# Routed experts' gate and up weights handled in two channel halves of each place of the ring

## The chip, the cores and the metric

The kernel runs on one core of a Trainium2 chip. The metric is the device time of one execution in microseconds (us); before the change it is the median of 3 runs. A profile of one execution gives the span from the first to the last instruction and the rows shown below.

## The reference

Two transformer blocks of width 1024 are applied to 256 tokens (batch 1). The first has two kinds of attention and then a mixture of 64 routed experts with 8 chosen for each token, beside one shared expert. The second has two gated feed-forward layers of width 2816 around another mixture of attentions. All is in float32. The change concerns the routed experts:

```python
def swiglu(x, w_gate, w_up, w_down):
    return (jax.nn.silu(x @ w_gate) * (x @ w_up)) @ w_down
...
    def body(acc, bidx):
        ...
        e = blk_expert[bidx]
        ye = swiglu(xt[rows], w_gate_e[e], w_up_e[e], w_down_e[e]) * wr[:, None]
        return acc.at[rows].add(ye.astype(acc.dtype)), None
```

Each expert has a gate and an up matrix of 1024x256 and a down matrix of 256x1024, 1 MiB each, so that 192 MiB of weights are read for this stage alone.

## The kernel before

The stage of the routed experts lies between about 285 and 767 us of the profiled execution. The rows (tokens) of an expert are gathered by a product with a 0/1 matrix; experts are put in order of size, and the work is cut into 28 turns, numbered 0 to 27. A turn fills the 128 rows of a PE pass: kinds P and B take one load, which is a pair of experts, kind Q takes two loads, which is four experts with 32 rows each. `KINDS = "PPQPPBPPQPPPBPPQPPBPPPPBPPPQ"`, so turns 2, 8, 15 and 27 take two loads and there are 32 loads of 6 MiB, numbered 0 to 31.

The weights go through `ring`, which has two places; load n goes to place n % 2. A place holds six units of 1 MiB (`UNIT` = 2048 floats on each of 128 partitions): gate of expert 0 and 1, up of expert 0 and 1, down of expert 0 and 1. In a gate or up unit each partition holds 8 channels of 256 numbers, 8 KB that lie together in memory, as well.

Everything waits by semaphores, and each engine runs its list in order. The sync engine (SP) issues all weight transfers on one queue, which serves them in that order. For a load it waits until PE has finished gate and up of the turn that used the place before (`used_gu`), and issues four transfers (L603); then for the down products of that turn (`y_ps`), and issues two (L612). Turn 2 takes load 2 with its down weights before load 3; later turns of two loads issue both loads' gate and up first, then both loads' down. Before a turn's transfers SP reads the experts' numbers from `order_i`, which is there at about 285 us; loads 0 and 1 go to fixed experts and are in flight before that.

PE in turn s (`body(s)`): `rows_gate_up(s)` (L2272: for each of the 8 channels, one product for each expert of the turn, into bank 4, 32 products for a pair), then gathering for a later turn (`fill`, L2247), adding the last turn's result to the tokens (`scatter`, L2309), `pick_t` (L2261), the transpose `rows_t` (L2282), and `rows_down(s)` (L2297). Turns 2 and 8 begin with the shared expert's products (L2210), turns 3 and 9 with its down part (L2222, L2230). ACT and DVE do the activation and the gating (L954, L1459), once all eight channels are summed. In the source:

```python
                if load >= 2:
                    sp.wait_ge(used_gu, 4 * (TURN_OF[load - 2] + 1))
...
                    for k in range(len(places) // 2):
                        pe.wait_ge(landed_gu[(load + k) % 2], 64 * ((load + k) // 2 + 1))
```

Of the kernel before, what the change touches and what calls it, by code (L numbers as in the profile page):

```python
# [127 lines left out]
def build(nc, a, out):  # L128
    ctx = ExitStack()
    with ctx:  # L130
# [190 lines left out]
        def bank(i):  # L321
            return ps[i // 2][:, i % 2, :]
# [15 lines left out]
        class Stream:  # L338
# [3 lines left out]
            def __init__(self, tag):  # L342
# [12 lines left out]
        in_ = {n: sem("in_" + n) for n in ("c", "x", "con", "ident", "bada", "relb", "bucket", "rpb",  # L355
                                           "tb", "nb", "mods", "g2r", "t1", "n1", "tw", "nw", "wrt", "rbias", "gains", "post",
# [3 lines left out]
        c_silu, c_wide = sem("c_silu"), sem("c_wide")  # L360
# [4 lines left out]
        tb_ps, tb_sb = sem("tb_ps"), sem("tb_sb")  # L365
# [10 lines left out]
        rt_tot, rt_flag, ordered = sem("rt_tot"), sem("rt_flag"), sem("ordered")  # L376
        w_back, w_there = sem("w_back"), sem("w_there")
        tok_hi = sem("tok_hi")
        landed_gu = [sem(f"landed_gu{i}") for i in range(2)]
# [89 lines left out]
        def if_over(eng, body):  # L469

            eng.wait_ge(rt_flag, 1)
# [16 lines left out]
        def _(sp):  # L488
# [63 lines left out]
            def spread_rows(r):  # L552

                sp.wait_ge(ada_rows, r + 1)
                sp.wait_ge(in_["n1"], 16)
                for j in range(4):
                    dst = mods[2 * r + j // 2][:, j % 2 * 512:j % 2 * 512 + 512]
                    for q in range(4):
                        sp.dma_start(dst[q:P:4, :], mod_rows[32 * j:32 * j + 32, :]).then_inc(in_["mods"], 16)

            for t in range(N_WIN):
                load_dense(G_WIN + t, w_in[:, :, t * 512:(t + 1) * 512])
                if t == 1 or t >= 3:
                    k = DC + 2 * max(t - 2, 0)
                    load_ada(k)
                    load_ada(k + 1)
                if t == 8:
                    spread_rows(1)
                if t == 5:

                    sp.wait_ge(in_["tw"], 16)
                    sp.dma_start(mb_bias, bass.AP(t_dram.tensor, 127, [[NH * BX - 1, P], [BX, NH], [1, T]]))\
                        .then_inc(in_["tb"], 16)
# [8 lines left out]
            sp.dma_start(w_rt, a["w_router"][0].rearrange("(p c) n -> p c n", c=DC)).then_inc(in_["wrt"], 16)  # L582
            sp.dma_start(rbias, a["router_bias"].to_broadcast([P, E])).then_inc(in_["rbias"], 16)
# [72 lines left out]
            sp.wait_ge(used_gu, 4 * N_TURN)  # L656
            sp.dma_start(pre1, a["ffn1_pre_g_2"].to_broadcast([P, D])).then_inc(in_["gains"], 16)
            def na_tables():

                sp.wait_ge(in_["nw"], 16)  # L660
# [48 lines left out]
        def _(pool):  # L709
# [42 lines left out]
            def double_roots():  # L752
# [15 lines left out]
            pool.wait_ge(tb_sb, 1)  # L768
            pool.dma_start(t_one, t_bias).then_inc(in_["t1"], 16)
            pool.wait_ge(in_["t1"], 16)  # L770
            pool.dma_start(t_dram, t_one.unsqueeze(0).to_broadcast([P, NH, BX])).then_inc(in_["tw"], 16)
# [3 lines left out]
                .then_inc(in_["rpb"], 16)  # L775
            pool.wait_ge(in_["rpb"], 16)
            pool.dma_start(n_one, rpb_pad).then_inc(in_["n1"], 16)
            pool.wait_ge(in_["n1"], 16)
            pool.dma_start(n_dram, n_one.unsqueeze(0).to_broadcast([64, NH, NR])).then_inc(in_["nw"], 16)
# [21 lines left out]
        def _(act):  # L801
# [128 lines left out]
            def sparse_phase():  # L930
# [78 lines left out]
            act.activation(c_sil, c_col, ACT.Silu).then_inc(c_silu, 1)  # L1009
# [10 lines left out]
            act.dma_start(relb_in[0:32, :], a["rel_bias_t"]).then_inc(in_["relb"], 16)  # L1020
            act.dma_start(bucket_in, a["buckets"]).then_inc(in_["bucket"], 16)
# [264 lines left out]
        def _(dve):  # L1286
# [116 lines left out]
            def sparse_phase():  # L1403
# [42 lines left out]
                def body(s):  # L1446
# [7 lines left out]
                    if s == 1:  # L1454
                        dve.wait_ge(rt_tot, 1)
                        dve.tensor_copy(over_i[0:1, 0:1], bank(7)[0:1, 0:1]).then_inc(rt_flag, 1)
# [50 lines left out]
            dve.wait_ge(c_silu, 1)  # L1507
            dve.tensor_copy(c_bc[:, :, :], c_sil.unsqueeze(2).to_broadcast([P, DC, 32])).then_inc(c_wide, 1)
# [60 lines left out]
            def sb_negabs(g):  # L1569
                z = of_group(z_sb, g)  # L1570
                dve.wait_ge(sb_zc, 2 * g + 2)
                if g == 0:
                    dve.wait_ge(in_["t1"], 16)
                dve.scalar_tensor_tensor(out=of_group(l_sb, g), in0=z, scalar=-1.0, in1=z, op0=ALU.mult, op1=ALU.min)\
                    .then_inc(sb_ab, 1)
# [56 lines left out]
            for j in range(N_WIN):  # L1632
                if j == 1:
                    dve.wait_ge(tb_ps, 1)
                    dve.tensor_copy(t_bias, bank(0)[0:NH, 0:BX]).then_inc(tb_sb, 1)
# [79 lines left out]
            dve.wait_ge(in_["rbias"], 16)  # L1715
# [82 lines left out]
            def over():  # L1798
# [6 lines left out]
                dve.wait_ge(w_back, 1)  # L1805
                dve.tensor_copy(w_over, bank(4)[:, 0:P].rearrange("p (b e) -> p b e", b=TB)).then_inc(w_there, 1)
                dve.wait_ge(w_there, 1)
# [193 lines left out]
        def _(pe):  # L2001
# [231 lines left out]
            def sparse_phase():  # L2233
# [31 lines left out]
                def rows_gate_up(s):  # L2265

                    _, places, load, groups, _ = TURNS[s]
                    for k in range(len(places) // 2):
                        pe.wait_ge(landed_gu[(load + k) % 2], 64 * ((load + k) // 2 + 1))
                    for c in range(DC):  # L2270
                        for i, (r, pair, j, at_) in enumerate(groups):
# [3 lines left out]
                            if c == DC - 1:  # L2275
                                last.then_inc(used_gu, 4 // len(groups))
# [39 lines left out]
                def body(s):  # L2316
# [23 lines left out]
                    if s == 1:  # L2340
# [3 lines left out]
                            .then_inc(rt_tot, 1)  # L2344
                        pe.wait_ge(rt_flag, 1)
# [158 lines left out]
            pe.wait_ge(c_wide, 1)  # L2504
# [106 lines left out]
            for j in range(N_WIN):  # L2611
# [12 lines left out]
                if j == 1:  # L2624
                    pe.wait_ge(in_["relb"], 16)
                    pe.wait_ge(in_["bucket"], 16)
                    pe.matmul(bank(0)[0:NH, 0:BX], relb_in, bucket_in, start=True, stop=True).then_inc(tb_ps, 1)
                if j >= 2:
                    pe.wait_ge(ev_v, EV_V[G_WIN + j - 2])
                if j == FIRST:  # L2630
                    pe.wait_ge(in_["con"], 16)
                    pe.wait_ge(tb_sb, 1)
# [32 lines left out]
            pe.wait_ge(in_["wrt"], 16)  # L2665
# [36 lines left out]
            def over():  # L2702
# [3 lines left out]
                pe.transpose(bank(4)[:, 0:P], w_past, ident).then_inc(w_back, 1)  # L2706
                pe.wait_ge(w_there, 1)
# [122 lines left out]
```

## Time and profile before

| | us |
|---|---|
| median of 3 runs | 1321.71 |
| lowest and highest run | 1319.38, 1323.28 |
| span of the profiled execution | 1317.2 |
| busy in it: PE, DVE, ACT | 1224.0, 541.9, 445.1 |

The page gives the profiled execution by its span only; the 4.5 us between span and median lie before the first and behind the last instruction, or between executions. Matmuls are pipelined and overlap in the rows, so a sum of busy times is no path. A chain of waits is followed back from the last instruction; a piece of it that reads "DMA" runs from the issue of the transfer to its landing.

### The profile page before, as it was taken

The page shows a single profiled execution, that of the slowest core. Times are in us where ns is not written, and L with a number is a line of the kernel's source. Part 1 is how long each engine was busy: PE and PEld are TensorE (multiplying, and loading weights), DVE is VectorE, ACT ScalarE, POOL GpSimd, SP SyncE. Part 2 cuts the span into 40 slices and gives each one's busy share as a digit, 9 for nine tenths or more (in the row PEclk, how much of TensorE's full clock was granted, in tenths as well). Part 3 has the DMA queues.
Part 4 walks back from the last instruction along what each step waited for, and adds up shares of the span by engine and source line. Part 5 has one row for each costly group of instructions (what it writes and reads, how often), then busy time and mean ns, then how long its engine had stood idle before and what let it go on. Part 6 is the DMA issues. An engine that isn't in the chain of part 4 may idle for free.

```text
span 1317.2 us, 16742 instructions
## 1 busy us (share of the span) xinstructions
PE 1224.0 (93%) x6726; PEld 855.7 (65%) x6726; DVE 541.9 (41%) x812; ACT 445.1 (34%) x657; POOL 44.5 (3%) x66
## 2 busy tenths in 40 slices
PE   4999999989999999789999779999999988999998
PEld 2877777754445444344455257888889867788886
DVE  1555546651111122111122165554566545544454
ACT  1345445321211122111122044444345545444332
POOL 0000000000000000000000020300010001000000
PEclk9899999989999999889999889999999979999999
DMA  9996655768999999999999998465615106455540
GB/s 372 363 363 230 223 200 184 286 250 351 372 421 421 412 421 421 405 398 421 421 420 421 407 270 259 158 212 185 228 46 192 64 1 224 156 196 187 186 137 32
DMA packets 115315, 359.54 MB, mean 273 GB/s; under 512 B 15092, under 2 KB 62629, under 8 KB 84334
## 3 DMA queue, kind: packets, MB, share of 16 engines
q1 hardware_dynamic: 113520, 352.71, 70.9%
q0 software_dynamic: 320, 3.46, 0.7%
q10 hardware_dynamic: 1406, 2.42, 0.6%
q8 instruction: 48, 0.79, 0.2%
q14 instruction: 21, 0.17, 0.0%
HBM read 355.37 MB, written 4.50 MB: 273 GB/s over the span
## 4 chain that ended last, share of the span: by engine, by line
PE 79%; DMA 10%; DVE 5%; ACT 2%; SPq 1%; issue 1%; POOL 0%; DVEq 0%; POOLq 0%; ACTq 0%
PE bank L2029 29%; PE bank L2272 14%; PE bank L2169 9%; DMA ring<-in_w_up_e 8%; PE bank L2297 6%; PE bank L2116 4%; PE bank L2247 4%; PE bank L2309 3%; DMA att<-in_w_ada 2%; PE bank L2380 1%; PE bank L2402 1%; PE bank L2085 1%; PE bank L2045 1%; PE bank L2158 1%; DMA raw_g<-in_ffn_w_gu 1%
## 5 line engine op out<-in xcount | busy, mean ns | idle before, releaser
L1301 DVE TENSOR_TENSOR g_lo<-raw_g,g_hi 128x2048 fp32r<-128x2048 f32 (+2 forms) x84 | 192.7, 2295 | 112.7 <-ACT g_hi L824 56.9
L2029 PE MATMUL bank<-g_hi,xt_hi 128*128 128x512 f32 (+1 forms) x576 | 231.2, 401 | 7.1 <-DVE xt_lo L1307 2.6
L2272 PE MATMUL bank<-ring,xg 128*64 128x512 f32 (+1 forms) x1152 | 205.1, 616 | 27.1 <-DMA ring<-in_w_up_e 27.1
L2029 PE MATMUL bank<-g_hi,xt_lo 128*128 128x512 f32 (+1 forms) x576 | 225.1, 391 | 0.0
L2029 PE MATMUL bank<-g_lo,xt_hi 128*128 128x512 f32 (+1 forms) x576 | 224.1, 389 | 0.0
L2272 PEld LDWEIGHTS bank<-ring,xg 128*64 128x64 f32 (+1 forms) x1152 | 64.7, 129 | 163.1 <-issue 159.4
L2029 PEld LDWEIGHTS bank<-g_hi,xt_hi 128*128 128x128 f32 x576 | 108.6, 189 | 35.5 <-issue 12.3
L2029 PEld LDWEIGHTS bank<-g_hi,xt_lo 128*128 128x128 f32 x576 | 108.4, 188 | 23.0
L2029 PEld LDWEIGHTS bank<-g_lo,xt_hi 128*128 128x128 f32 x576 | 108.6, 189 | 20.5
L824 ACT ACTIVATE g_hi<-raw_g 128x2048 fp32r<-128x2048 f32 (+3 forms) x42 | 78.2, 1865 | 77.5 <-PE bank L2029 39.4
L2297 PE MATMUL bank<-ring,a_t 128*64 128x512 f32 (+1 forms) x576 | 102.6, 598 | 1.4 <-DVE pickT L1412 0.9
L1459 DVE SCALAR_TENSOR_TENSOR arena<-arena,w_row_of,bank 128x256 f32<-128x256 f32 x28 | 13.4, 480 | 203.6 <-ACT arena L954 203.6
L822 ACT ACTIVATE g_hi<-raw_g 128x2048 fp32r<-128x2048 f32 x44 | 84.1, 1913 | 20.3 <-DMA raw_g<-in_ffn_w_gu 11.8
L954 ACT ACTIVATE arena<-bank 128x256 f32<-128x256 f32 x28 | 10.8, 385 | 222.4 <-PE bank L2272 222.4
L1444 DVE TENSOR_TENSOR y_lo<-bank,y_hi 128x512 fp32r<-128x512 f32 x56 | 38.7, 692 | 104.3 <-ACT y_hi L940 104.3
L1321 DVE TENSOR_TENSOR d_lo<-raw_d,d_hi 128x2048 fp32r<-128x2048 f32 x20 | 48.5, 2423 | 45.7 <-ACT d_hi L868 45.7
L2297 PEld LDWEIGHTS bank<-ring,a_t 128*64 128x64 f32 (+1 forms) x576 | 30.4, 125 | 53.0 <-issue 48.8
L2169 PE MATMUL bank<-d_hi,at_hi 128*128 128x512 f32 x160 | 62.5, 390 | 0.0
L2169 PE MATMUL bank<-d_hi,at_lo 128*128 128x512 f32 x160 | 62.3, 389 | 0.0
L2169 PE MATMUL bank<-d_lo,at_hi 128*128 128x512 f32 x160 | 62.2, 389 | 0.0
L940 ACT ACTIVATE y_hi<-bank 128x512 fp32r<-128x512 f32 x56 | 33.4, 597 | 70.4 <-PE bank L2297 70.4
L868 ACT ACTIVATE d_hi<-raw_d 128x2048 fp32r<-128x2048 f32 x20 | 38.3, 1917 | 52.5 <-PE bank L2169 52.5
(370 smaller groups left out, 1665.6 us busy)
## 6 DMA issues: line engine op xcount, KB each, us to landing
ring<-in_w_gate_e SPq DMA_DIRECT2D x64, 1024.0 KB, 12.8
ring<-in_w_up_e SPq DMA_DIRECT2D x64, 1024.0 KB, 16.8
ring<-in_w_down_e SPq DMA_DIRECT2D x64, 1024.0 KB, 16.2
raw_g<-in_ffn_w_gu SPq DMA_DIRECT2D x44, 1024.0 KB, 9.4
raw_g<-in_w_in SPq DMA_DIRECT2D x26, 1024.0 KB, 7.7
raw_d<-in_ffn_w_down SPq DMA_DIRECT2D x22, 1024.0 KB, 5.0
ada_d<-in_w_ada SPq DMA_DIRECT2D x16, 1024.0 KB, 7.0
raw_g<-in_w_out SPq DMA_DIRECT2D x8, 1024.0 KB, 5.3
```

What stands on the lines that cost most here:

```text
L822: act.activation(dst, raw_gated(g, u), ACT.Copy).then_inc(S.hi_g, 1)
L824: act.activation(g_hi[:, u, 0:cols], raw_dense(g, u)[:, 0:cols], ACT.Copy).then_inc(S.hi_g, 1)
L1301: dve.tensor_tensor(lo, raw, hi.bitcast(F32), ALU.subtract).then_inc(S.lo_g, 1)
L1321: dve.tensor_tensor(d_lo[:, :], raw_d[:, d % 2, :], d_hi[:, :].bitcast(F32), ALU.subtract)\
L1444: dve.tensor_tensor(lo, bank(5 + m), hi.bitcast(F32), ALU.subtract).then_inc(y_v, 1)
L2029: last = pe.matmul(out_, src[s][:, c, b * P:(b + 1) * P], w((g_hi, g_lo)[m], i), start=start and i == 0 and k == 0, stop=stop and i == len ...
L2116: last = pe.matmul(bank(banks[m // 2])[:, (m % 2) * T:(m % 2 + 1) * T], (g_hi, g_lo)[w][:, u, c * 512 + m * P:c * 512 + (m + 1) * P], (xt_ ...
L2169: last = pe.matmul(bank(2 * b + m), a_hl[i][:, c, b * P:(b + 1) * P], d_hl[w][:, c * D + m * 512:c * D + (m + 1) * 512], start=False, stop ...
L2247: last = pe.matmul(fill_bank(n)[:, i * 4 * ROWS:(i + 1) * 4 * ROWS], tok[k][:, b, c, :], pick[:, q % 2, b, :], start=k == 0 and b == 0 and ...
L2272: last = pe.matmul(bank(4)[r, :].rearrange("p (g n) -> p g n", g=2), xg[:, s // 2 % 2, c, at_:at_ + r.stop - r.start], gate_up_raw(pair, j ...
L2297: last = pe.matmul(bank(5 + m)[r, :], a_t[:, c, r], down_raw(pair, j, c, m), start=c == 0, stop=c == 1, skip_group_check=True)
L2309: last = pe.matmul(bank(2 * b + m), pickT[:, s % 2, b * P:(b + 1) * P], t[:, m * 512:(m + 1) * 512], start=False, stop=s == N_TURN - 1 and ...
```

## The change

The gate and up part of a load is issued as eight transfers of half a unit: first channels 0 to 3 of gate and up of both experts, then channels 4 to 7. Each half has its own wait of SP for the place (the half turn before that frees it), its own semaphore for the landing, and its own wait of PE, ahead of channel 0 and ahead of channel 4. PE reports the place's halves used after channel 3 and after channel 7, so that `used_gu` counts 8 a turn, and those that wait for a turn's end wait for 8 s + 8. A partition's piece in one transfer is 4 KB where it was 8 KB. The down weights are loaded as before. In the same diff several semaphores elsewhere are merged (for example `c_silu` and `c_wide` into `c_ready`, and those of the router's weights and bias into `router`), with the counts waited for raised accordingly.

```diff
-        landed_gu = [sem(f"landed_gu{i}") for i in range(2)]
+        landed_gu = [[sem(f"landed_gu{i}{j}") for j in range(2)] for i in range(2)]
...
             def load_gate_up(load, pair):
 
-                if load >= 2:
-                    sp.wait_ge(used_gu, 4 * (TURN_OF[load - 2] + 1))
-                for g, n in enumerate(("w_gate_e", "w_up_e")):
-                    for j in range(2):
-                        at_ = (2 * g + j) * UNIT
-                        sp.dma_start(ring[:, load % 2, at_:at_ + UNIT], one_row(n, pair[j], DC))\
-                            .then_inc(landed_gu[load % 2], 16)
+                for half in range(2):
+                    if load >= 2:
+                        sp.wait_ge(used_gu, 8 * TURN_OF[load - 2] + 4 * half + 4)
+                    for g, n in enumerate(("w_gate_e", "w_up_e")):
+                        for j in range(2):
+                            at_ = (2 * g + j) * UNIT + half * (UNIT // 2)
+                            sp.dma_start(ring[:, load % 2, at_:at_ + UNIT // 2],
+                                         one_row(n, pair[j], DC)[:, half * (UNIT // 2):(half + 1) * (UNIT // 2)])\
+                                .then_inc(landed_gu[load % 2][half], 16)
...
-            sp.wait_ge(used_gu, 4 * N_TURN)
+            sp.wait_ge(used_gu, 8 * N_TURN)
...
-                    act.wait_ge(used_gu, 4 * s + 4)
+                    act.wait_ge(used_gu, 8 * s + 8)
...
-            pe.wait_ge(in_["wrt"], 16)
+            pe.wait_ge(in_["router"], 32)
...
-                    for k in range(len(places) // 2):
-                        pe.wait_ge(landed_gu[(load + k) % 2], 64 * ((load + k) // 2 + 1))
                     for c in range(DC):
+                        for k in range(len(places) // 2 if c % (DC // 2) == 0 else 0):
+                            pe.wait_ge(landed_gu[(load + k) % 2][c // (DC // 2)], 64 * ((load + k) // 2 + 1))
                         for i, (r, pair, j, at_) in enumerate(groups):
                             last = pe.matmul(bank(4)[r, :].rearrange("p (g n) -> p g n", g=2),
                                              xg[:, s // 2 % 2, c, at_:at_ + r.stop - r.start], gate_up_raw(pair, j, c),
                                              start=c == 0, stop=c == DC - 1, skip_group_check=True)
-                            if c == DC - 1:
+                            if c % (DC // 2) == DC // 2 - 1:
                                 last.then_inc(used_gu, 4 // len(groups))
```

## Rows read from the trace of the kernel before

**Rows 1.** The page's head, and GB/s moved in 40 slices of the span.

```profile
span 1317.2 us, 16742 instructions
...
GB/s 372 363 363 230 223 200 184 286 250 351 372 421 421 412 421 421 405 398 421 421 420 421 407 270 259 158 212 185 228 46 192 64 1 224 156 196 187 186 137 32
```

**Rows 2.** The chain that ended last, whole span, shares by engine.

```profile
PE 79%; DMA 10%; DVE 5%; ACT 2%; SPq 1%; issue 1%; POOL 0%; DVEq 0%; POOLq 0%; ACTq 0%
```

**Rows 3.** PE's waits from 285 to 770 us: total, times, longest.

```profile
PE bank L2272 <- DMA ring<-in_w_up_e: 27.1, 7, 8.8
```

**Rows 4.** Windows: length, busy of PE, PEld, DVE, ACT, POOL, PEclk, DMA share, GB/s.

```profile
325.00:333.00 8.00, 8.00 (x74) 3.57 (x64) 0.48 (x1) 0.73 (x2) 0.00 (x0) 1.00 0.25 74
350.00:436.00 86.00, 83.63 (x506) 43.94 (x506) 16.50 (x48) 16.24 (x32) 0.00 (x0) 1.00 1.01 421
557.00:563.00 6.00, 6.00 (x48) 3.58 (x41) 0.48 (x1) 0.98 (x2) 0.00 (x0) 1.00 0.59 197
563.00:757.00 194.00, 181.03 (x1042) 85.67 (x1045) 35.62 (x97) 35.73 (x68) 0.00 (x0) 0.96 1.01 420
...
749.00:751.00 2.00, 2.00 (x13) 0.45 (x9) 0.00 (x0) 0.00 (x0) 0.00 (x0) 0.50 1.04 434
```

**Rows 5.** The chain in order of time, routed stage: start us, us, what.

```profile
310.73 13.52 DMA ring<-in_w_up_e
324.39 7.07 PE bank L2272 x64
...
606.34 7.00 PE bank L2272 x64
...
621.51 7.02 PE bank L2272 x32
...
735.83 12.50 DMA ring<-in_w_up_e
748.46 9.29 PE bank L2272 x64
```

**Rows 6.** The timeline at the stage's start and end: start us, us, instructions.

```profile
284.95 7.09 PE L2272 MATMUL bank<-ring,xg 128*64 128x512 f32 x32
...
292.27 0.89 SPq L603 DMA_DIRECT2D ring<-in_w_gate_e  x2
...
309.31 0.85 SPq L603 DMA_DIRECT2D ring<-in_w_gate_e  x2
...
321.78 0.29 DVE L1401 TENSOR_TENSOR arena<-arena,bank 128x128 f32<-128x128 f32 x1 [2.63 <-ACT arena L923]
...
335.99 3.64 PE L2297 MATMUL bank<-ring,a_t 128*32 128x512 f32 x32
...
760.53 3.64 PE L2297 MATMUL bank<-ring,a_t 128*32 128x512 f32 x32 [0.47 <-ACT a_t L958]
```

**Rows 7.** Issue to landing of L612's two transfers from 339.72, then from 741.56 us.

```profile
DMA to landing us min/median/max: 8.0/9.0/10.0
...
DMA to landing us min/median/max: 14.2/15.3/16.3
```

**Rows 8.** A window (columns of rows 4) in which `w_out_2` alone lands, in 4 KB pieces.

```profile
1010.00:1011.50 1.50, 1.50 (x16) 1.50 (x15) 1.14 (x1) 0.85 (x2) 0.00 (x0) 1.00 1.00 412
```

**Rows 9.** Transfers: count, KB each, median us to landing; 8 KB pieces first, then 4 KB.

```profile
raw_d<-in_ffn_w_down SPq DMA_DIRECT2D x22, 1024.0 KB, 5.0
...
raw_g<-in_w_out SPq DMA_DIRECT2D x4, 1024.0 KB, 4.9
...
arena<-in_w_down_sh SPq DMA_DIRECT2D x1, 512.0 KB, 9.8
d_sh<-in_w_down_sh SPq DMA_DIRECT2D x1, 512.0 KB, 10.9
```

**Rows 10.** SP's timeline where those two of 512 KB are issued.

```profile
233.08 0.43 SPq L632 DMA_DIRECT2D arena<-in_w_down_sh  x1
233.55 0.76 SPq L632 DMA_DIRECT2D d_sh<-in_w_down_sh  x1
```

More of the change, by code:

```diff
@@ L354, in build @@
         h_ready, x_ready = sem("h_ready"), sem("x_ready")
-        in_ = {n: sem("in_" + n) for n in ("c", "x", "con", "ident", "bada", "relb", "bucket", "rpb",
-                                           "tb", "nb", "mods", "g2r", "t1", "n1", "tw", "nw", "wrt", "rbias", "gains", "post",
+        in_ = {n: sem("in_" + n) for n in ("c", "x", "con", "ident", "bada", "buckets", "n_table",
+                                           "t_table", "tb", "nb", "mods", "g2r", "router", "gains", "post",
                                            "outg", "ff2g")}
@@ L359, in build @@
         set_up = sem("set_up")
-        c_silu, c_wide = sem("c_silu"), sem("c_wide")
+        c_ready = sem("c_ready")
         landed_ada = [sem(f"landed_ada{i}") for i in range(4)]
@@ L364, in build @@
         mod_col, w0_half = sem("mod_col"), sem("w0_half")
-        tb_ps, tb_sb = sem("tb_ps"), sem("tb_sb")
+        tb_made = sem("tb_made")
         ev_a, ev_v = sem("ev_a"), sem("ev_v")
@@ L469, in if_over @@
         def if_over(eng, body):
-            eng.wait_ge(rt_flag, 1)
+            eng.wait_ge(rt_beyond, 2)
             beyond = eng.value_load(over_i[0:1, 0:1], min_val=0, max_val=T * E)
@@ L554, in spread_rows @@
                 sp.wait_ge(ada_rows, r + 1)
-                sp.wait_ge(in_["n1"], 16)
+                sp.wait_ge(in_["n_table"], 32)
                 for j in range(4):
@@ L581, in _ @@
             sp.wait_ge(h_ready, 4)
-            sp.dma_start(w_rt, a["w_router"][0].rearrange("(p c) n -> p c n", c=DC)).then_inc(in_["wrt"], 16)
-            sp.dma_start(rbias, a["router_bias"].to_broadcast([P, E])).then_inc(in_["rbias"], 16)
+            sp.dma_start(w_rt, a["w_router"][0].rearrange("(p c) n -> p c n", c=DC)).then_inc(in_["router"], 16)
+            sp.dma_start(rbias, a["router_bias"].to_broadcast([P, E])).then_inc(in_["router"], 16)
             def moe_gate_up(s, it):
@@ L766, in _ @@
             roots(0, 2)
[L768 to L771, printed above, removed]
+            pool.wait_ge(tb_made, 2)
+            pool.dma_start(t_one, t_bias).then_inc(in_["t_table"], 16)
+            pool.wait_ge(in_["t_table"], 16)
+            pool.dma_start(t_dram, t_one.unsqueeze(0).to_broadcast([P, NH, BX])).then_inc(in_["t_table"], 16)
             link(pool.memset(rpb_pad, 0.0))
             pool.dma_start(rpb_pad.rearrange("h (r c) -> h r c", r=7)[:, :, 48:79], a["na_rpb_2"][0][:, 4:11, :])\
[L775 to L779, printed above, removed]
+                .then_inc(in_["n_table"], 16)
+            pool.wait_ge(in_["n_table"], 16)
+            pool.dma_start(n_one, rpb_pad).then_inc(in_["n_table"], 16)
+            pool.wait_ge(in_["n_table"], 32)
+            pool.dma_start(n_dram, n_one.unsqueeze(0).to_broadcast([64, NH, NR])).then_inc(in_["n_table"], 16)
             block_roots(1)
@@ L1008, in _ @@
             act.wait_ge(in_["c"], 16)
-            act.activation(c_sil, c_col, ACT.Silu).then_inc(c_silu, 1)
+            act.activation(c_sil, c_col, ACT.Silu).then_inc(c_ready, 1)
             squares(0, [x[:, b, :] for b in range(TB)], in_["x"], 16, lambda i: h[:, i, :])
@@ L1019, in _ @@
             act.dma_start(con[:, P:C_END], a["con"][:, P:C_END]).then_inc(in_["con"], 16)
-            act.dma_start(relb_in[0:32, :], a["rel_bias_t"]).then_inc(in_["relb"], 16)
-            act.dma_start(bucket_in, a["buckets"]).then_inc(in_["bucket"], 16)
+            act.dma_start(relb_in[0:32, :], a["rel_bias_t"]).then_inc(in_["buckets"], 16)
+            act.dma_start(bucket_in, a["buckets"]).then_inc(in_["buckets"], 16)
             bias_rows(1, ADA_ROUNDS)
@@ L1454, in body @@
                     if s == 1:
-                        dve.wait_ge(rt_tot, 1)
-                        dve.tensor_copy(over_i[0:1, 0:1], bank(7)[0:1, 0:1]).then_inc(rt_flag, 1)
+                        dve.wait_ge(rt_beyond, 1)
+                        dve.tensor_copy(over_i[0:1, 0:1], bank(7)[0:1, 0:1]).then_inc(rt_beyond, 1)
                     dve.wait_ge(sp_silu, s + 1)
@@ L1504, in attend2 @@
                     sm_finish(8 + s - 3)
-            dve.wait_ge(c_silu, 1)
-            dve.tensor_copy(c_bc[:, :, :], c_sil.unsqueeze(2).to_broadcast([P, DC, 32])).then_inc(c_wide, 1)
+            dve.wait_ge(c_ready, 1)
+            dve.tensor_copy(c_bc[:, :, :], c_sil.unsqueeze(2).to_broadcast([P, DC, 32])).then_inc(c_ready, 1)
             def ada_sum(r):
@@ L1633, in _ @@
                 if j == 1:
-                    dve.wait_ge(tb_ps, 1)
-                    dve.tensor_copy(t_bias, bank(0)[0:NH, 0:BX]).then_inc(tb_sb, 1)
+                    dve.wait_ge(tb_made, 1)
+                    dve.tensor_copy(t_bias, bank(0)[0:NH, 0:BX]).then_inc(tb_made, 1)
                 if j:
@@ L1714, in _ @@
                                          op0=ALU.mult, op1=ALU.add).then_inc(h_ready, 1)
-            dve.wait_ge(in_["rbias"], 16)
+            dve.wait_ge(in_["router"], 32)
             def sel01(b):
@@ L1804, in over @@
                 transposed(0, OV, 4)
-                dve.wait_ge(w_back, 1)
-                dve.tensor_copy(w_over, bank(4)[:, 0:P].rearrange("p (b e) -> p b e", b=TB)).then_inc(w_there, 1)
-                dve.wait_ge(w_there, 1)
+                dve.wait_ge(w_moved, 1)
+                dve.tensor_copy(w_over, bank(4)[:, 0:P].rearrange("p (b e) -> p b e", b=TB)).then_inc(w_moved, 1)
+                dve.wait_ge(w_moved, 2)
                 gated_phase("over", weight=w_over)
@@ L2343, in body @@
                         pe.matmul(bank(7)[0:1, 0:1], st[:, 52:53], ones[:, 0:1], start=True, stop=True)\
-                            .then_inc(rt_tot, 1)
-                        pe.wait_ge(rt_flag, 1)
+                            .then_inc(rt_beyond, 1)
+                        pe.wait_ge(rt_beyond, 2)
                     if more:
@@ L2503, in _ @@
             pe.wait_ge(set_up, 3)
-            pe.wait_ge(c_wide, 1)
+            pe.wait_ge(c_ready, 2)
             ada_chunks(0, 4)
@@ L2624, in _ @@
                 if j == 1:
-                    pe.wait_ge(in_["relb"], 16)
-                    pe.wait_ge(in_["bucket"], 16)
-                    pe.matmul(bank(0)[0:NH, 0:BX], relb_in, bucket_in, start=True, stop=True).then_inc(tb_ps, 1)
+                    pe.wait_ge(in_["buckets"], 32)
+                    pe.matmul(bank(0)[0:NH, 0:BX], relb_in, bucket_in, start=True, stop=True).then_inc(tb_made, 1)
                 if j >= 2:
@@ L2705, in over @@
                 pe.wait_ge(OV.xt_lo, 4)
-                pe.transpose(bank(4)[:, 0:P], w_past, ident).then_inc(w_back, 1)
-                pe.wait_ge(w_there, 1)
+                pe.transpose(bank(4)[:, 0:P], w_past, ident).then_inc(w_moved, 1)
+                pe.wait_ge(w_moved, 2)
                 pe.sem_inc(OV.used_d, 1)
```

12 lines of the change are left out of this document (6 added, 6 removed).

## Prediction

> **What bounds the kernel now.** I read the page's head first: the GB/s in slices of 33 us. From the 12th to the 22nd slice, the stage of the routed experts, the transfers run at 398 to 421 GB/s and nowhere else do they stay there [rows 1]. Then the chain's shares: PE 79%, DMA 10% [rows 2]; and PE's waits inside the stage: 27.1 us in 7 waits, all on `ring`, the longest 8.8 [rows 3]. So the chain runs mostly over PE, and still the gain to be had is not on PE. The windows show why: from 350 to 436 and from 563 to 757 us the DMA share is 1.01 at 420 to 421 GB/s [rows 4]. A load of 6 MiB (6.29 MB) takes 6.29 / 421 = 14.94 us; a turn of one load takes 621.51 - 606.34 = 15.17 us [rows 5]. The two are within 2% of each other. The four turns with two loads need 29.9 us of transfers and give PE about as much to do as the others, and there PE waits. Over 30 loads (2 to 31) the transfers need 30 x 14.94 = 448 us, of the 466 from their first issue at 292.27 to the last landing [rows 6, 7]: the stream of transfers is the bound, and what counts is when it starts, where it stops, and how fast a MiB goes.
>
> Where it stops in the profile: before 292.27 (SP waits for the end of turn 0's gate and up, 284.95 + 7.09 [rows 6]); 325 to 333 us at a share of 0.25; 557 to 563 us at 0.59, that is 2.5 us idle [rows 4]. The last landing is 741.99 + 16.3 = 758.3 [rows 7] (the second of the two is issued 0.4 us behind the first). PE's last down products start at 760.53, and what ended their wait was ACT's `a_t`, not the landing [rows 6].
>
> **The change, part by part.**
>
> *Earlier release.* The half of a plain turn's gate and up is 7.07 / 2 = 3.5 us. SP may issue channels 0 to 3 that much earlier. For load 2: 284.95 + 3.5 + 0.2 = 288.7 in place of 292.27. Load 3 likewise, 3.5 us ahead of its 309.31 [rows 6].
>
> *Turn 2.* It begins at 324.39, when load 3's last gate and up transfer lands (310.73 + 13.52) [rows 5]. PE itself is ready after the shared expert's gating, 321.78 + 0.29, say 322.2 [rows 6]. Half 0 of load 3 is issued at 305.8; behind the down weights of load 2, which are still issued when turn 0's down products end, near 302, and land near 310, its 2 MiB land near 316 and half 1 near 321, before PE needs it at 325.7. So turn 2 starts at 322.2: 2.2 us earlier. What is late next is load 4: its half 0 is issued at turn 2's middle, 325.9, in place of 331.7, and lies in the hole of 325 to 333; its down weights wait for turn 2's down products and (the end of 335.99 + 3.64 [rows 6]) and go out at 339.72 - 2.2 = 337.5, landing at 337.5 + 2.5 + 5.0 = 345.0. (2.5 us from issue to first data: a lone MiB lands after 5.0 us [rows 9], 2.5 of it data.) In the profile they landed at 340.15 + 10.0 = 350.2 [rows 7]. Of the 5.2 us gained, 2.2 is turn 2's start and 3.0 is that gate and up of load 4 no longer stand in the queue ahead of them.
>
> *From there the stream does not stop.* After 345.0 each half is freed well before its place in the queue comes up. The tightest is load 19, freed by turn 15 (loads 17 and 18): the stream would reach it at 345.0 + 14 x 15.16 = 557.2, and half of turn 15 is over near 547. Before, it was issued after the whole of turn 15, hence the 2.5 us idle at 557 to 563; these go.
>
> *The price: pieces of 4 KB.* A window in which only 4 KB pieces move shows 412 GB/s at a full share [rows 8], against 421 for 8 KB [rows 4]. Gate and up of a load: 4.194 MB / 412 = 10.18 us in place of 9.96; a load 15.16 in place of 14.94. Over the 27 loads from 5 to 31 that is +5.9 us. Bounds: from below, lone transfers of 1 MiB take 5.0 us in 8 KB pieces and 4.9 in 4 KB pieces [rows 9], so the price may be nothing; from above, the two transfers of 512 KB land at 233.08 + 9.8 = 242.9 and 233.55 + 10.9 = 244.5 [rows 9, 10], 1.6 us apart where 412 GB/s gives 1.27. That would be 216 halves x 0.33 = +71 us, but other traffic may lie in the one interval. I take the window, since it is a full queue as here.
>
> *The sum.* Before, from 350.2 to 758.3 are 408.1 us for 27 loads: 27 x 14.94 = 403.4, 2.5 idle, and 2.2 in late single landings. After: 345.0 + 27 x 15.16 (409.3) + 1.6 (of the 2.2, between none and all) = 755.9. Now the landing of the last down weights is what PE's last down products wait for: gate and up of load 31 land 10 us earlier, and with half 0 done by then turn 27's gate and up end near 750, `a_t` near 753. They start at 756.0, not at 760.53: **-4.5 us**. All that follows (the sums to the tokens, the norm, the feed-forward layer) hangs on them and moves along; its weights are issued after turn 27's gate and up and land earlier too. Span 1317.2 - 4.5 = 1312.7. The runs' median is 4.5 above the span, so 1321.7 - 4.5 = **1317.2**.
>
> *Costed at nothing.* Four more issues a load on SP: two take about 0.9 us, so ten take 4.7 of the 15.17 us of a turn; SP has nothing else to do, and no transfer is delayed while the stream is backed up. If it were starved, up to 1.9 us a load would show. PE's extra wait ahead of channel 4: behind it stand gathering, scatter, the transpose, and ACT and DVE after them; between the turns of two loads PE runs some us behind the landings, so it is met already; at turns 15, 16 and 27 it does stop PE, but there PE waits for the stream anyhow and now does half a turn's products meanwhile. The merged semaphores ask for the same events; where PE now waits for the router's bias too, that is issued right behind the weights, long before PE's output projection is done.
>
> *A rule of the skill against it.* The transfers of 1 MiB in the queue run at 421 GB/s [rows 4], and one alone takes 5.0 us for 2.5 us of data [rows 9]: in the queue the other 2.5 is hidden. The Trainium skill, DMA: Bandwidth & Descriptors, Bandwidth, advises batching to 1 MiB or more because each transfer has a fixed cost; by its figures (2.0 us plus bytes at 436 GB/s) splitting adds 8.0 us a load, an estimate of +216 us if nothing hid it. By the rows above nearly all of it is hidden.
>
> **The rivals.**
>
> *A. Halved transfers cost more than the window says (slower).* The place is each of the 216 half transfers from load 5 on; the price 216 x what each takes over 1.27 us. From 1.29 the gain is gone, from 1.31 the kernel is 0.3% slower; at 1.35 it would be 216 x 0.08 = +17 over my sum, 1334. For it speak the 1.6 us above; against it 412 GB/s in a full window and 4.9 beside 5.0 us. Chance 0.20.
>
> *B. 4 KB pieces cost nothing (more gain).* Then 27 x 0.22 = 5.9 more: 1311.3. For it: 4.9 beside 5.0; against: the window. The skill's same page (Specifications) has pieces from 512 B at line rate. By that rule it comes out so, 1311.3. Chance 0.12.
>
> *C. The clock takes the gain (no change).* After PE's 6.9 us of waiting ahead of turn 27 its granted clock is 0.50 in the window from 749 to 751 [rows 4], the lower of its two levels, 1.2 GHz, and gate and up take 9.29 us in place of 7.07 [rows 5]. After the change PE waits ahead of turn 27, again ahead of channel 4, and some 3 us for the last down weights. If the clock is low then, the last 3.64 us of products [rows 6] take up to twice that: -4.5 + 3.6 = -0.9, 1320.8. Against it: after the 2.3 us of waiting at turn 2 the products ran at 7.07 [rows 5]. Chance 0.13.
>
> *D. The start gains nothing.* If load 2's and 3's halves queue so that turn 2 starts as before, load 4's down weights land 3.0 earlier, not 5.2: 1319.4. Chance 0.10.
>
> My forecast keeps 0.45. **The numbers.** 0.3% is 4 us, about what a measurement can tell from none. The forecast's own spread, from lateness 0 to 2.2 and the window's 412 read as 410 to 415, is 1314 to 1320: six parts in ten of it beyond 4 us. Faster 0.45 x 0.6 + 0.12 + a little of C and D = 0.43; slower 0.20; the same 0.37. The range reaches from B, 1310, to A at 1.32 us a half, 1328.
>
> **What would show it.** In the profile after: L603's first issue near 288.7; turn 2's L2272 from 322.2; no window under a share of 1.00 from 345 to 755; 8 of L603 to a load, landing 1.27 us apart, 412 to 421 GB/s there; a last landing near 756 with L2297 waiting for `ring` from down weights, not for ACT. A mean of 1.31 us apart, or a stream that stops after 345, would make the prediction wrong.

## The result and the profile after

| | before | after |
|---|---|---|
| median of the runs compared, us | 1320.4 (19 runs) | 1324.1 (19 runs) |
| lowest and highest run, us | 1318.74, 1325.35 | 1322.32, 1326.04 |
| span of the profiled execution, us | 1317.2 | 1323.3 |
| own time of the profiled execution, us | not given | 1325.18 |

The ratio is 1.0021 with a 95% interval of 1.0012 to 1.003, so the changed kernel is slower by 0.21%, 1.6 to 4.0 us. (The two medians differ by 3.7 us; what follows goes by the ratio, 2.8 us.) That is within the 0.3% that the prediction counted as the same, but on the other side of no change from the 1317.2 us that it forecast. In the runs from here on, the profiled execution's own time is 1.8 to 1.9 us above its span. If that held before the change too, the execution profiled there took some 1319.1 us, an estimate, and of the 4.5 us between its span and the median 2.6 are only that it was a quick one.

The page's head and its GB/s by slices, which answer to [rows 1]:

```profile
span 1323.3 us, 17050 instructions
...
GB/s 371 341 368 242 209 206 189 253 309 338 385 413 412 413 414 412 413 412 412 413 414 412 406 268 238 155 217 182 230 51 191 64 1 222 151 197 183 186 141 32
```

From the 12th to the 22nd slice no slice falls below 412, where before two fell to 398 and 405; but none reaches 421 either. The stream no longer stops, and it runs slower throughout. The chain's shares by engine, against [rows 2]:

```profile
PE 70%; SPq 13%; DMA 7%; DVE 5%; ACT 2%; issue 2%; POOL 0%; DVEq 0%; POOLq 0%; ACTq 0%
```

SP's queue (SPq) has 13% of the chain where it had 1%. That isn't time in which SP waits for PE; the waits of SP and of PE inside the stage (total, times, longest) say so. SP before:

```profile
SPq L603 <- PE bank L2272: 187.9, 27, 16.2
SPq L612 <- PE bank L2297: 143.1, 24, 7.8
```

SP and PE after, L604 and L614 being the issues that were L603 and L612, L2274 and L2299 the products that were L2272 and L2297:

```profile
SPq L614 <- PE bank L2299: 36.5, 7, 8.3
SPq L604 <- PE bank L2274: 36.3, 12, 9.6
...
PE bank L2274 <- DMA ring<-in_w_up_e: 21.0, 7, 9.3
PE bank L2299 <- DMA ring<-in_w_down_e: 6.6, 3, 3.8
```

SP waited 331 us for PE and now waits 73. It may now issue well ahead, and the issues themselves stretch: two take 0.88 us together at 290.52, when the queue is empty, and one alone takes 1.03 us in the chain's rows below. That it is the full queue which holds them back is argued from that, not shown. PE's waits came to 27.1 us [rows 3] and are 27.6 now: some for gate and up went, 6.6 for down weights came. The windows that answer to [rows 4] (the same columns):

```profile
350.00:436.00 86.00, 84.53 (x511) 43.67 (x508) 16.52 (x48) 16.63 (x33) 0.00 (x0) 1.00 1.02 413
439.00:547.00 108.00, 99.63 (x568) 48.36 (x566) 20.59 (x56) 21.41 (x41) 0.00 (x0) 0.98 1.02 412
563.00:745.00 182.00, 169.56 (x970) 80.47 (x970) 34.12 (x90) 34.89 (x67) 0.00 (x0) 0.99 1.02 413
...
762.50:765.00 2.50, 2.42 (x12) 0.68 (x16) 0.00 (x0) 0.00 (x0) 0.00 (x0) 0.50 1.07 355
765.00:767.00 2.00, 2.00 (x16) 0.63 (x12) 0.07 (x1) 0.60 (x1) 0.00 (x0) 0.50 1.10 349
```

The DMA share is 1.02, a full stream, and moves 412 to 413 GB/s where it moved 420 to 421. The last two rows belong to the end of the stage, when transfers for the next layer are under way already; they are shown for the granted clock. The chain there, in order of time:

```profile
739.48 1.03 SPq L614
740.60 1.04 SPq L614
741.73 20.71 DMA ring<-in_w_down_e
762.44 0.14 issue
762.58 6.63 PE bank L2299 x32
```

The last down weights land at 741.73 + 20.71 = 762.44 us, PE stands idle for them, and its last down products take 6.6 us, where they took 3.64 [rows 6]: their granted clock is 0.50, the lower level of 1.2 GHz. (They are 16 products in 32 rows: the trace keeps two rows for one product in float32. Likewise gate and up of a pair are 16 products in 32 rows, not 32 products.)

**Where the stage starts.** Its first product is at 286.63 us, 1.7 later than the 284.95 of before [rows 6]. In the other profiles of this study it lies between 284.8 and 287.8, and four kernels that have the merged semaphores too start within 0.3 us of the kernel before. So I take it for scatter of single profiles and subtract it ("less 1.7") when the two are compared:

| us | predicted | profile after, less 1.7 |
|---|---|---|
| first L604 issue | 288.7 | 290.52 - 1.7 = 288.8 |
| turn 2 starts | 322.2 | 323.89 - 1.7 = 322.2 |
| down weights of load 4 landed | 345.0 | 349.3 - 1.7 = 347.6 |
| last down weights landed | 755.9 | 762.44 - 1.7 = 760.7 |
| last down products take | 3.64 | 6.56 |
| they end | 759.6 | 769.14 - 1.7 = 767.4 |

A single profile doesn't bear the last digit of this. The kernels with four loads halved (below) are alike up to the last turn; in their two profiles the stage starts at 285.18 and at 286.65 us, and turn 2 at 323.83 and 323.93. Differences of this table that are below some 1.5 us show little.

The spans of the two profiles differ by 6.1 us: 1.7 ahead of the stage's first product, 3.3 from there to the end of the last down products, and 1.1 behind them. This account explains the 3.3. The stretch behind is 553.0 us long before the change and 553.9 to 557.2 in the ten experiments' profiles. Whether the one profile of before is a quick one there, or something that all the changed kernels share costs time, was not settled.

In between PE ran ahead as meant. Turn 16 starts each half when that half has landed (the first two rows), at 568.71 where the whole began at 573.11, and turn 17 starts at 585.38 where it started at 591.06 (all times here as read, without the 1.7):

```profile
568.71 3.65 PE L2274 MATMUL bank<-ring,xg 128*64 128x512 f32 x16 [1.48 <-DMA ring<-in_w_up_e]
573.72 3.65 PE L2274 MATMUL bank<-ring,xg 128*64 128x512 f32 x16 [1.36 <-DMA ring<-in_w_up_e]
585.38 5.21 PE L2274 MATMUL bank<-ring,xg 128*64 128x512 f32 x21
```

But most of the lead of 5.7 us is given back: turn 27 starts at 747.54 instead of 748.46 [rows 5], after PE has waited 9.3 us for the stream. A lead of PE was worth nothing here, where the stream sets the end.

### The profile page after: what moved, and what is told of

It reads as the page before. It is cut to its first block, busy times and chain, and to the rows that moved or that the text cites. A ratio compares the mean times of both kernels' runs of the same rounds, so it can differ in the third digit from the quotient of the medians.

```text
span 1323.3 us, 17050 instructions
## 1 busy us (share of the span) xinstructions
PE 1231.3 (93%) x6723; PEld 858.7 (65%) x6726; DVE 542.2 (41%) x812; ACT 445.6 (34%) x657; POOL 45.4 (3%) x66
## 4 chain that ended last, share of the span: by engine, by line
PE 70%; SPq 13%; DMA 7%; DVE 5%; ACT 2%; issue 2%; POOL 0%; DVEq 0%; POOLq 0%; ACTq 0%
PE bank L2031 29%; SPq L604 9%; PE bank L2171 9%; PE bank L2274 7%; DMA ring<-in_w_down_e 5%; PE bank L2299 5%; PE bank L2118 4%; SPq L614 3%; PE bank L2249 2%; PE bank L2311 2%; PE bank L2047 1%; PE bank L2382 1%; PE bank L2404 1%; DMA arena<-in_w_ada 1%; PE bank L2087 1%
## 5 line engine op out<-in xcount | busy, mean ns | idle before, releaser
L2274 PE MATMUL bank<-ring,xg 128*64 128x512 f32 (+1 forms) x1152 | 203.7, 611 | 22.9 <-DMA ring<-in_w_up_e 21.0
L2274 PEld LDWEIGHTS bank<-ring,xg 128*64 128x64 f32 (+1 forms) x1152 | 61.8, 127 | 160.2 <-issue 146.5
L2299 PE MATMUL bank<-ring,a_t 128*64 128x512 f32 (+1 forms) x576 | 105.6, 620 | 7.5 <-DMA ring<-in_w_down_e 6.6
L826 ACT ACTIVATE g_hi<-raw_g 128x2048 fp32r<-128x2048 f32 (+3 forms) x42 | 78.2, 1865 | 77.7 <-PE bank L2031 39.4
L2299 PEld LDWEIGHTS bank<-ring,a_t 128*64 128x64 f32 (+1 forms) x576 | 31.5, 128 | 60.8 <-issue 57.6
```

What stands on the lines that cost most here:

```text
L826: act.activation(g_hi[:, u, 0:cols], raw_dense(g, u)[:, 0:cols], ACT.Copy).then_inc(S.hi_g, 1)
L2274: last = pe.matmul(bank(4)[r, :].rearrange("p (g n) -> p g n", g=2), xg[:, s // 2 % 2, c, at_:at_ + r.stop - r.start], gate_up_raw(pair, j ...
L2299: last = pe.matmul(bank(5 + m)[r, :], a_t[:, c, r], down_raw(pair, j, c, m), start=c == 0, stop=c == 1, skip_group_check=True)
```

## The experiments

Ten kernels were run, each compared with the kernel before on the same chip. Ratios and gains in us are to it, with the 95% interval behind the ratio.

**The semaphores and counts alone.** The changed kernel's merged semaphores and `used_gu` counting 8 a turn, with no load halved (`HALVED_LOADS = ()`, in the form shown under "four loads halved" below).

> The changed kernel with its merged semaphores and its count of 8 a turn, but each gate and up transfer whole (1 MiB, 8 KB pieces), waited for and given back whole. Theory 1 (all of the loss lies in the routed stage) expects the time of the kernel before, within 0.1%. The rival (the stage begins 1.7 us later in the changed kernel's profile because merged semaphores make something wait) expects 1.7 us or 0.13% more than before.

Measured 1321.39 us, 1.0007 (0.999 to 1.0023); windows 421, 419 and 421 GB/s. So these parts of the diff cost 0.9 us, from -1.3 to +3.0: nothing that can be told, as priced, though the rival's 1.7 us isn't excluded either.

**Half transfers with whole waits.** Nothing of the half turns' gain is left, only the price of the eight transfers:

```diff
-                        sp.wait_ge(used_gu, 8 * TURN_OF[load - 2] + 4 * half + 4)
+                        sp.wait_ge(used_gu, 8 * TURN_OF[load - 2] + 8)
...
-                        for k in range(len(places) // 2 if c % (DC // 2) == 0 else 0):
-                            pe.wait_ge(landed_gu[(load + k) % 2][c // (DC // 2)], 64 * ((load + k) // 2 + 1))
+                        for k in range(len(places) // 2 if c == 0 else 0):
+                            for half in range(2):
+                                pe.wait_ge(landed_gu[(load + k) % 2][half], 64 * ((load + k) // 2 + 1))
```

> The changed kernel with transfers in two channel halves of 4 KB pieces, but both halves' place waited for at the turn's end and both landings waited for ahead of channel 0: the price without the gain. At 413 GB/s, as in the changed kernel's profile, against 421, a load of 6.29 MB takes 0.3 us more, 27 loads 8.2 us; the last down landing had 2.2 us in hand before, and PE's last down products at the low clock would cost 2.9: 8.2 - 2.2 + 2.9 = +9 us over before. If the prediction's own price holds (0.22 us a load) +6.6.

Measured 1337.14 us, 1.0118 (1.0093 to 1.0144): **+15.6 us**, far more than the 5.9 of the prediction's sum. Its windows (columns as above):

```profile
350.00:436.00 86.00, 84.63 (x470) 44.73 (x470) 16.50 (x48) 16.25 (x32) 0.00 (x0) 0.98 1.02 413
439.00:547.00 108.00, 104.80 (x611) 51.67 (x604) 18.79 (x51) 20.22 (x39) 0.00 (x0) 0.99 0.99 395
563.00:745.00 182.00, 175.30 (x1022) 84.26 (x1024) 33.21 (x90) 34.75 (x66) 0.00 (x0) 0.97 1.00 403
563.00:573.00 10.00, 9.72 (x66) 2.90 (x67) 0.00 (x0) 0.11 (x1) 0.00 (x0) 0.74 0.81 337
```

Where nothing stops the stream it runs at the 413 GB/s of the changed kernel; around the turns of two loads it also stops, since those turns' places come free late. It stops for longer than in the kernel before, behind turn 8 and behind turn 15:

```profile
443.00:448.00 5.00, 5.00 (x43) 2.53 (x36) 0.48 (x1) 0.80 (x2) 0.00 (x0) 1.00 0.38 120
570.00:575.00 5.00, 5.00 (x42) 2.77 (x35) 0.48 (x1) 0.98 (x2) 0.00 (x0) 1.00 0.38 137
```

These are some 6 us without transfers, where the kernel before lost 2.5 behind turn 15 [rows 4] and about 0.4 behind turn 8 (a share of 0.89 from 436 to 439 us). Load 4's down weights also land 4.6 us later, at 354.76. So the price has several parts: the rate, longer stops and a later start.

**Count or size.** Two kernels, both with whole waits, take the two properties of a half transfer apart. The first keeps eight transfers a load and pieces of 8 KB, by giving each transfer every second partition; the second keeps four transfers of 1 MiB, each written as two pieces of 4 KB a partition, into the two halves of a place laid out half by half:

```diff
+                    part = slice(half, P, 2)
...
+                            sp.dma_start(ring[part, load % 2, at_:at_ + UNIT], one_row(n, pair[j], DC)[part, :])\
```

> Eight transfers of 512 KB a load in whole 8 KB pieces, waits whole as in e2_pieces, but each transfer takes every second partition, so that all 128 partitions are spread over as before (e3_rows, with 64 neighbouring partitions a transfer, moved at 221 to 243 GB/s and so told nothing of the number of transfers). Theory 1 (the size of the pieces costs) expects the kernel before, +0 to +1 us. Theory 2 (the number of transfers costs) expects +16 us, the time of e2_pieces.

```diff
+                        dst = ring[:, load % 2, 0:4 * UNIT].rearrange("p (h i n) -> p h i n", h=2, i=4)[:, :, 2 * g + j, :]
+                        sp.dma_start(dst, one_row(n, pair[j], DC).rearrange("p (h n) -> p h n", h=2))\
```

> The opposite: four transfers of 1 MiB a load as before, waits whole, but each partition's 8 KB go to two places of 4 KB (the ring's gate and up part is laid out half by half). Theory 1 expects e2_pieces, +16 us or, for the 4 KB packets alone (163 ns for 4 KB against 314 for 8 KB, 0.3 us a load), +8 to +12. Theory 2 expects the kernel before.

The count alone: 1324.27 us, 1.0022 (1.0006 to 1.0038), +2.9 us, above the 0 to 1 that was expected. The size alone: 1331.07 us, 1.0079 (1.006 to 1.0097), +10.4 us, as expected. The window from 350 to 436 us of the one and then of the other:

```profile
350.00:436.00 86.00, 83.99 (x501) 44.14 (x500) 16.50 (x48) 16.25 (x32) 0.00 (x0) 1.00 1.01 421
```

```profile
350.00:436.00 86.00, 81.88 (x494) 43.73 (x494) 16.50 (x48) 16.25 (x32) 0.00 (x0) 1.00 1.02 413
```

In this window twice as many transfers run at the rate of before; pieces half as long do not, in transfers of whatever number. So the rate is a matter of the piece's length, and with it two thirds of the price: 10.4 of the 15.6 us, and the count's 2.9 make 13.3. Neither figure is rate alone: from 563 to 573 us both kernels stop (shares of 0.95 and 0.81). At 413 against 421 GB/s, 27 loads take 7.8 us more, an estimate; the rest of the 10.4 is not taken apart.

**Eight transfers of 64 neighbouring partitions.** My first attempt at "count alone", with `part = slice(half * (P // 2), (half + 1) * (P // 2))`.

> As e2_pieces, eight transfers of 512 KB a load, but each is 64 partitions of whole 8 KB pieces. Theory 1 (the size of the pieces costs) expects the time of the kernel before, +0 to +1 us. Theory 2 (the number of transfers costs: SP's queue was full at 11 to 13 outstanding, and one DMA engine some us behind the others) expects the time of e2_pieces, +9 us.

Measured 1692.78 us, 1.2827 (1.2773 to 1.2881). Nothing like it was expected, and it says nothing about the count, since the rate broke down altogether:

```profile
350.00:436.00 86.00, 54.94 (x292) 25.47 (x292) 8.90 (x24) 9.75 (x19) 0.00 (x0) 0.82 0.91 221
```

**What wins the 13 us back.** Between half transfers with whole waits (+15.6) and the changed kernel (+2.8) lie SP's wait by halves and PE's wait by halves. One kernel keeps the first alone, with PE's whole wait as in the diff above; the other keeps PE's alone, with SP's whole wait.

> SP waits by halves as in the changed kernel, PE waits for both halves ahead of channel 0. If the early issue of transfers is what wins back the 13 us between all halves with whole waits (1337.1) and the changed kernel (1324.1): within 2 us of 1324. If PE's wait by halves wins them: near 1337. Mine: early issue wins most, since with it the queue holds work at every turn's end: 1325 to 1328, PE's wait by halves being worth at most the landing of four transfers (some 7 us) once, at the last turn.

> SP waits for the whole turn's end before all eight transfers of a load, PE waits by halves. If the early issue wins the 13 us: near 1337. If PE's wait by halves does: near 1324. Mine: 1331 to 1335; the stream still stops at the start of the stage and where a turn takes two loads, since nothing is issued before a turn's end.

SP's alone: 1326.69, 1.0041 (1.0025 to 1.0057). PE's alone: 1327.08, 1.0044 (1.0032 to 1.0056). Each wins back about 10 of the 13 us, SP's as expected; PE's I had expected to win 2 to 6. The window from 563 to 573 us shows it, SP's alone first, then PE's alone:

```profile
563.00:573.00 10.00, 8.02 (x62) 4.85 (x61) 3.40 (x10) 3.15 (x6) 0.00 (x0) 1.00 1.02 377
```

```profile
563.00:573.00 10.00, 7.29 (x48) 2.39 (x48) 1.38 (x2) 1.20 (x2) 0.00 (x0) 1.00 1.03 407
```

Either keeps the stream from stopping (share 1.02 and 1.03, against 0.81). PE's wait by halves must do it another way, as I read the program: the turn begins earlier, so it ends and frees the whole place earlier. The two gains are for the most part one gain, the stop, and can't be added.

**The clock at the end.** The changed kernel with 26 products of constants put ahead of the last down products (`warm(26, 7)` in turn 27), which keep PE at work while it would wait. They are added work, and show as 52 rows.

> The changed kernel with 26 products of 128x128 into the unused bank 7 ahead of the last turn's wait for its down weights, whose result nobody reads. If the lower clock of the last 32 down products (6.56 us where they took 3.64) is part of the loss, 2 to 3 us less than the changed kernel; if not, the same as the changed kernel or up to 1 us more.

Measured 1325.14 us, 1.0035 (1.002 to 1.005), where 2 to 3 us less than the changed kernel were expected if the clock was part of the loss. The timeline:

```profile
759.03 5.97 PE L2019 MATMUL bank<-con 128*128 128x128 f32 x52
764.93 3.64 PE L2299 MATMUL bank<-ring,a_t 128*32 128x512 f32 x32
```

With no idle time ahead of them the last down products take 3.64 us again, at a granted clock of 1.00. The cause of the 6.6 is thus shown; the gain isn't, because in this profile the weights landed at 763.85, 1.4 us later than in the other, and the added products ran 1.1 us beyond that.

**Four loads halved.** If the price is paid by each load and the gain made at few places, then only loads 2, 3 and 4 (the start) and 19 (behind turn 15) should be halved:

```diff
+HALVED_LOADS = (2, 3, 4, 19)
...
-                for half in range(2):
+                halves = 2 if load in HALVED_LOADS else 1
+                n_ = UNIT // halves
+                for half in range(halves):
```

> The changed kernel, but only loads 2, 3, 4 and 19 are halved (those ahead of which the stream stopped in the kernel before); the other 28 are whole. If the early release gains 5 us by load 4 and 2.5 at load 19, and the price lies in the pieces of the steady stretch, the last landing comes 7 us earlier at 421 GB/s: 6 to 8 us less than before (PE's last gate and up, still at the low clock, ends with its own 12 us behind the landing). If the gain was not there, the time of the kernel before.

Measured 1320.28 us, 1.0007 (0.999 to 1.0025): the price is gone, and of the 6 to 8 us expected no gain is left in the time. The windows of this kernel:

```profile
340.00:350.00 10.00, 9.90 (x38) 3.63 (x40) 0.49 (x1) 0.04 (x1) 0.00 (x0) 1.00 0.97 370
...
435.00:438.00 3.00, 3.00 (x27) 1.80 (x20) 0.48 (x1) 0.71 (x2) 0.00 (x0) 1.00 0.50 194
...
563.00:573.00 10.00, 10.00 (x67) 3.65 (x67) 2.70 (x8) 2.18 (x4) 0.00 (x0) 1.00 1.01 368
```

The down weights of load 4 landed at 349.4 us (350.2 before), although they were issued at 339.2, as the prediction has it: the 10 us in which they land move 370 GB/s, in the changed kernel 363, before 424. The stop behind turn 15 is gone, but behind turn 8, whose place load 11 takes, the stream now stops for 1.5 us (the second row; a share of 0.91 before, 1.01 in the changed kernel): the choice of loads missed it.

Part of the gain is there in the profile all the same. The last down weights land at 756.33 us where they landed at 758.28, and PE's last down products start at 757.76 where they started at 760.53, held up by ACT's `a_t`. What undoes it is the stretch behind the stage, 556.3 us against 553.0, of which the section on the result speaks.

**The same with the clock held.** The last kernel with 20 such added products ahead of turn 27's gate and up.

> e6_some with 20 products into the unused bank 7 ahead of the last turn's wait for its gate and up weights, so that PE does not idle there. If the clock's fall costs 2.2 us in the last turn's gate and up (9.29 us where 7.07), another 2 us less than e6_some; if it is hidden or falls anyway, the same.

Measured 1318.51 us, 0.999 (0.9978 to 1.0002), with an interval that still holds no change. Turn 27's gate and up took 9.6 us all the same. It is the lowest median of the study, and shown to be faster neither than the kernel before nor than the last one.

## Why the prediction was wrong

**Right.** The stream of transfers bounds the kernel; the first issue follows the stage's first product after 3.9 us (7.3 before), where 3.75 was forecast; turn 2 waits for the shared expert's gating and no longer for load 3; the stop behind turn 15 is gone (from 557 to 563 us the share is 1.01 where it was 0.59 [rows 4]); PE's last wait is for down weights; the merged semaphores cost nothing that shows; the stream stays full with eight issues a load, so SP is no limit; and twice the count keeps the rate of 421 GB/s in the window shown. The 2.2 us gained at turn 2 may be owed to the halves only in small part: with all loads whole it starts 37.5 us behind the stage's first product, where it is 37.3 with the halves and 39.4 in the profile of before.

**Wrong in three terms of the sum**, which together turn -4.5 into +3.3 us in the stage. The measured difference of the whole is 2.8, between 1.6 and 4.0.

1. *Landing of load 4's down weights, "337.5 + 2.5 + 5.0 = 345.0".* They were issued when predicted, 337.5 (339.21 less 1.7), and landed at 347.6: **2.6 us** lost. Load 4's own half transfers are all landed at 341.72, 2.5 us after the issue; the delay lies behind that. In the window from 340 to 350 us, at a share of 0.99, 363 GB/s move where 424 did, that is 0.61 MB or 1.4 us less. With load 5 whole, in the kernel with four loads halved, it is the same (370), so the length of what follows isn't the cause. Why transfers that meet an almost empty queue go at this rate is open; the term took two rows of lone transfers [rows 9] for a case that they don't cover. Rival D's 3.0 us earlier instead of 5.2 came nearest to the 2.6 that it is, but by another way: D had turn 2 start no earlier.

2. *"The price: pieces of 4 KB ... a load 15.16".* The prediction took 412 GB/s for the 4 KB pieces [rows 8] and 421 for the down weights, a mean of 415. The whole mix runs at 413, which leaves 409 for the 4 KB pieces, an estimate with 421 for the rest: 6.29 / 413 = 15.23 us a load, and from 349.3 to 762.44 us there are 413.1 us for 27 loads, 15.30 each. The terms were 409.3 + 1.6; measured are 411.2 at the windows' rate and 1.9 of lateness: **2.2 us** more. Over the half transfers this makes (15.30 - 4.98) / 8 = 1.29 us each, just where rival A put the point at which the gain is gone.

   What the lateness in both terms is made of can be seen closer. A transfer raises its semaphore in 16 steps as its parts land, and the trace keeps the time of each. From the first to the last of the 32 steps of a load's two down transfers it is, in us:

   | | before | after |
   |---|---|---|
   | load 4 | 350.17 - 346.05 = 4.1 | 349.31 - 343.63 = 5.7 |
   | load 31 | 758.28 - 753.88 = 4.4 | 762.44 - 754.66 = 7.8 |

   The parts run further and further apart in the changed kernel, and the last one is what PE waits for. Of the 2.6 us lost at load 4, 1.6 are this wider spread, and the 1.9 of lateness up to load 31 are its growth by 2.1. The prediction had no term for it. With PE's wait by halves alone the spread at load 31 is 7.7 us, with all loads whole 4.5, with whole waits and half transfers 6.3; what drives it is open.

3. *The clock, "they start at 756.0", taking 3.64.* PE idles 3.8 us for the last landing and its products run at 0.50: **2.9 us**. This is rival C, and here only the time of one group was at stake; the experiment with added products shows the cause. The prediction held against C that products after 2.3 us of waiting at turn 2 had run at full speed [rows 5] (PE stood idle there for 2.95 us, the gating included). After 3.8 us of waiting here, and after 3.5 in the kernel with PE's wait by halves, they did not (5.30 us there).

2.6 + 2.2 + 2.9 = 7.7, and -4.5 + 7.7 = +3.2; with rounding the table above gives +3.3. So the outcome is A in a mild form and C at once, with a start that gained no more than in D. I had weighed the rivals as if one alone would happen, while C needs nothing but the wait that my own forecast brings about: its 0.13 was the poorest number of the prediction. The other side of it is luck: that the time came out within 0.3% of before, which had 0.37, is two large effects that nearly cancel, and not a small one.

**The price that was hidden in it.** Had the halves' waits not been there, the smaller pieces and doubled count would have cost 15.6 us and not 6, with the stream stopping for longer at the turns of two loads. The gain of the halves was therefore large, some 13 us, and was spent on the pieces that make it possible. B (pieces for nothing) is refuted by the size-alone kernel, +10.4 us. The rule that would give B, pieces from 512 B at line rate (the Trainium skill, DMA: Bandwidth & Descriptors, Specifications), does not hold to the 2% that matter here: 421 GB/s with all in 8 KB pieces, 413 with two thirds of the bytes in 4 KB pieces. The +216 us that the prediction estimated from the Trainium skill was for the 108 more transfers of loads 5 to 31. The Trainium skill gives the advice to batch in the section that the prediction names, but the 2.0 us for a transfer in another (DMA: Bandwidth & Descriptors, Anatomy of one DMA — SWDGE (gpsimd) path), as a fit for transfers that GpSimd issues, where SP issues them here. The count alone, 128 more transfers, cost 2.9 us, so in a full queue such a cost is nearly all hidden.

**Open.** The rate behind an almost empty queue, and the growing spread of a transfer's parts; why size and count together cost 2.3 us more than the two added (the intervals allow for it to be nothing); what lies behind the stage's differences between profiles; and whether a kernel between these, with loads 11 and 20 halved too, is truly faster than before. With load 11 whole the stream stops behind turn 8; with load 20 whole turn 17 waits 4.21 us for it, starts at 586.98 where the changed kernel has 585.38, and takes 9.74 us. That was not tried.

## What to carry to other kernels

Where a stream of weights is the bound, a finer hand-over buys back stops only, and each byte pays for it: count the us of stops that there are (here 2.5 in the middle and a few at the start) against the rate lost on every load, and keep the pieces of a partition long. To split only the transfers at which the stream stops took the price away here, but brought no gain that could be measured; look for stops that move elsewhere. Expect one gain where several waits are relaxed around the same stop. When a change lets PE overtake the stream, price its next group at the lower clock.

## What the runs showed of the hardware

- Two thirds of the bytes in pieces of 4 KB a partition against all in 8 KB, at a full DMA share: 413 against 421 GB/s, whether in transfers of 512 KB or of 1 MiB.
- Transfers over 64 neighbouring partitions were slow: 221 GB/s from 350 to 436 us at a share of 0.91, and 245 from 439 to 547 us at a share of 1.01. Over every second partition, as many bytes in pieces as long moved at 421.
- PE idle for 3.8 us, then the last down products in 6.6 us at a granted clock of 0.50; without the idle time 3.64 us at 1.00; after 2.95 us idle at turn 2, gate and up in 7.07 us at 1.00.
- A DMA share near 1 doesn't mean full speed: 363 and 370 GB/s at 0.99 and 0.97 in the 10 us after the queue had almost run empty, against 424; and 368 at 1.01 from 563 to 573 us, behind turn 15, in the kernel with four loads halved.
- The 16 parts of a transfer drift apart: the 32 steps of load 31's two down transfers spread over 7.8 us in the changed kernel and 4.4 before.
